# Layer norms whose variance is inverted before its root is taken, and a head norm that keeps its rows as four token quarters

## What is computed

```python
def layernorm(x, g, b):          # after the convolution, over 768 channels
    mu = jnp.mean(xf, axis=-1, keepdims=True)
    var = jnp.mean(jnp.square(xf - mu), axis=-1, keepdims=True)
    y = (xf - mu) * lax.rsqrt(var + LN_EPS)

def layer_norm(x, g, b):         # second block, over 1024 features
    ...
    return ((x32 - mu) * lax.rsqrt(var + LN_EPS) * g + b)

def rms_norm(x, g):              # over the 128 features of one head
    ms = jnp.mean(jnp.square(x32), axis=-1, keepdims=True)
    return (x32 * lax.rsqrt(ms + LN_EPS) * g)

def odd_mixer(...):
    o = diff_attention(q, k, v, lam)             # 8 heads of 128
    o = rms_norm(o, subln_g) * (1.0 - lambda_init)
    return o.reshape(b, s, DIFF_W) @ w_out

def second_block(...):
    for i in range(DEPTH):
        x = layer_norm(ALPHA * x + (1.0 + g_m) * y, ln_mix_g[i], ln_mix_b[i])
        h = x * (1.0 + sc_f) + sh_f
        y = swiglu(h, w_gate[i], w_up[i], w_down[i])
        x = layer_norm(ALPHA * x + (1.0 + g_f) * y, ln_ffn_g[i], ln_ffn_b[i])
```

## Time and profile before

| | |
|---|---|
| median of 3 runs | 2707.3 us (2707.06 to 2709.83) |
| the profiled execution's own time | 2703.21 us |
| its span in the trace | 2701.5 us |
| PE busy | 2552.7 us (94%), 12225 matmul records |
| DVE busy | 1549.3 us (57%), 2243 instructions |
| ACT busy | 1051.2 us (39%), 1596 instructions |
| granted clock of PE over the span | 0.97 of full |

### The profile page before, as it was taken

How to read it: one execution, slowest core, us unless ns; L and a number is a source line. 1 busy time by engine, 2 the same in 40 slices (tenths; PEclk the granted TensorE clock), 3 DMA queues, 4 the chain that set the end, 5 groups by cost and what they waited for, 6 DMA issues and landing times.

```text
span 2701.5 us, 30620 instructions
## 1 busy us (share of the span) xinstructions
PE 2552.7 (94%) x12225; PEld 1983.1 (73%) x12225; DVE 1549.3 (57%) x2243; ACT 1051.2 (39%) x1596; POOL 70.9 (3%) x145
## 2 busy tenths in 40 slices
PE   7798999999998999999999899999999989999998
PEld 5466777777865777777777567888878756788886
DVE  5876587777355467767657555333364765533335
ACT  5235332335445432323544535222244663522223
POOL 2000001010000000000000000000000000000000
PEclk9898999999999999999999999999999998999998
DMA  5121356563312235645231022333223111333321
GB/s 168 47 94 32 88 161 203 156 187 101 95 56 71 78 109 182 177 154 169 83 94 63 1 60 81 94 94 94 82 75 94 47 47 53 88 94 94 94 82 43
DMA packets 327836, 262.32 MB, mean 97 GB/s; under 512 B 13426, under 2 KB 312630, under 8 KB 327696
## 3 DMA queue, kind: packets, MB, share of 16 engines
q1 hardware_dynamic: 312000, 206.07, 25.8%
q0 software_dynamic: 15440, 54.25, 6.3%
q10 hardware_dynamic: 256, 0.07, 0.0%
HBM read 258.23 MB, written 2.12 MB: 96 GB/s over the span
## 4 chain that ended last, share of the span: by engine, by line
PE 71%; PEld 8%; DVE 8%; ACT 5%; issue 4%; DVEq 3%; DMA 1%; ACTq 0%; PEldq 0%
PE ps L396 43%; PEld ps L396 6%; PE ps L410 6%; PE ps L414 6%; PE ps L418 6%; PE ps L1308 2%; PE ps L1868 2%; DVE wL L362 2%; PE ps L1339 1%; PE ps L2348 1%; ACT tmpB L1384 1%; DVEq L896 1%; PE ps L1322 1%; DVE tmpA L905 1%; ACT tmpA L869 1%
## 5 line engine op out<-in xcount | busy, mean ns | idle before, releaser
L362 DVE TENSOR_TENSOR wL<-raw,wH 128x2048 fp32r<-128x2048 f32 (+1 forms) x185 | 415.3, 2245 | 120.0 <-ACT wH L348 113.9
L348 ACT ACTIVATE wH<-raw 128x2048 fp32r<-128x2048 f32 (+1 forms) x185 | 345.3, 1868 | 245.5 <-PE ps L396 106.2
L396 PE MATMUL ps<-hH,wH 128*128 128x512 f32 x1656 | 427.6, 400 | 5.0 <-issue 1.9
L396 PE MATMUL ps<-hL,wH 128*128 128x512 f32 x1656 | 427.6, 400 | 0.0
L396 PE MATMUL ps<-hH,wL 128*128 128x512 f32 x1656 | 424.6, 398 | 0.0
L396 PEld LDWEIGHTS ps<-hH,wH 128*128 128x128 f32 x1656 | 308.1, 188 | 87.1 <-issue 13.2
L396 PEld LDWEIGHTS ps<-hL,wH 128*128 128x128 f32 x1656 | 310.8, 189 | 79.5 <-issue 6.5
L396 PEld LDWEIGHTS ps<-hH,wL 128*128 128x128 f32 x1656 | 308.9, 188 | 77.2 <-issue 4.8
L869 ACT ACTIVATE tmpA<-ff_up,cols 128x512 f32<-128x512 f32 x88 | 67.0, 808 | 255.8 <-DVEq L896 255.8
L410 PE MATMUL ps<-gH,wH 128*128 128x512 f32 x480 | 153.3, 409 | 10.3 <-ACT wH L348 7.4
L931 DVE TENSOR_TENSOR tmpB<-ps,tmpB 128x512 f32<-128x512 f32 x44 | 30.4, 692 | 231.0 <-PE ps L396 231.0
(11 more groups left out here) (353 smaller groups left out, 3317.7 us busy)
## 6 DMA issues: line engine op xcount, KB each, us to landing
raw<-w_up SPq DMA_DIRECT2D x132, 512.0 KB, 5.2
mod_ring<-w_mod POOLq DMA_DIRECT2D x96, 512.0 KB, 4.5
raw<-w_down SPq DMA_DIRECT2D x32, 1024.0 KB, 5.3
raw<-w_gate SPq DMA_DIRECT2D x44, 512.0 KB, 4.0
raw<-w_down SPq DMA_DIRECT2D x16, 768.0 KB, 4.5
raw<-w_in_even SPq DMA_DIRECT2D x9, 1024.0 KB, 5.2
raw<-w_out SPq DMA_DIRECT2D x8, 1024.0 KB, 5.2
raw<-w_in_odd SPq DMA_DIRECT2D x16, 512.0 KB, 4.6
```

The costliest lines, as they stand in the source:

```text
L348: last = act.activation(wH[:, st.part, 0:st.size], raw[:, st.slot, 0:st.size], ACT.Copy)
L362: last = dve.tensor_tensor(wL[:, st.part, 0:st.size], raw[:, st.slot, 0:st.size], wH[:, st.part, 0:st.size].bitcast(F32), ALU.subtract)
L396: last = pe.matmul(dst, left, right, start=(t == 0 and k == 0), stop=(t == 2 and k == self.kt - 1))
```

## The change

In the five layer norms, epsilon is added to the variance by DVE's clipping instruction, which now does two operations; DVE inverts the variance right behind it; ACT then takes the root of the inverse, without a bias, and PE's second spread waits for ACT (`roots`) and no longer for DVE. The semaphore `centred` goes. The root mean square norm keeps its order.

The head norm uses the layer norms' layout: `sum_quarters` forms the means of a batch in four quarters of 32 rows and 128 columns, root and inversion work on 128 x 128 blocks, and `spread_quarters`, which has a new argument for the row, spreads head n from row n of each quarter. The tensor `pick` and the eight instructions that fill it (line 1575) go. The diff, cut to its core (`ConvNorm` has the same edits in its `tensor` and `scalar` methods as `NormParts`, and the reservations of `centred` are gone):

```diff
@@ -956,10 +955,11 @@
-        def spread_quarters(pe, bank, src):
+        def spread_quarters(pe, bank, src, row=0):
             for g in range(QT):
-                last = pe.matmul(ps[:, bank, g * P:g * P + P], ident[:, GROUP * g:GROUP * g + 1].broadcast_to([P, P]), src, start=True, stop=True)
+                r = GROUP * g + row
+                last = pe.matmul(ps[:, bank, g * P:g * P + P], ident[:, r:r + 1].broadcast_to([P, P]), src, start=True, stop=True)
             return last
...
@@ -1046,7 +1046,10 @@
                     spread_quarters(pe, 6, quarter_mean).then_inc(spread_out.sem, 1)
-                pe.wait_ge(inverted.sem, self.inverted0 + 1)
+                if self.bname:
+                    pe.wait_ge(roots.sem, self.root0 + 1)
+                else:
+                    pe.wait_ge(inverted.sem, self.inverted0 + 1)
                 spread_quarters(pe, 7, quarter_inv).then_inc(spread_out.sem, 1)
@@ -1054,8 +1057,8 @@
                     act.activation(quarter_square, ps[:, 6, 0:P], ACT.Square).then_inc(squares.sem, 1)
-                    act.wait_ge(centred.sem, self.centred0 + 1)
-                    act.activation(quarter_std, quarter_var, ACT.Sqrt, bias=eps_ln).then_inc(roots.sem, 1)
+                    act.wait_ge(inverted.sem, self.inverted0 + 1)
+                    act.activation(quarter_inv, quarter_std, ACT.Sqrt).then_inc(roots.sem, 1)
                 else:
@@ -1097,11 +1100,14 @@
                     dve.drain()
-                    dve.tensor_scalar(quarter_var, quarter_var, 0.0, None, ALU.max).then_inc(centred.sem, 1)
+                    dve.tensor_scalar(quarter_var, quarter_var, 0.0, LN_EPS, ALU.max, ALU.add)
+                    dve.drain()
+                    dve.reciprocal(quarter_std, quarter_var).then_inc(inverted.sem, 1)
                     dve.wait_ge(spread_out.sem, self.spread0 + 1)
                     self.centre(dve, 0)
-                dve.wait_ge(roots.sem, self.root0 + 1)
-                dve.reciprocal(quarter_inv, quarter_std).then_inc(inverted.sem, 1)
+                else:
+                    dve.wait_ge(roots.sem, self.root0 + 1)
+                    dve.reciprocal(quarter_inv, quarter_std).then_inc(inverted.sem, 1)
                 self.centre(dve, 1)
@@ -1494,6 +1500,9 @@
+            def quarters(self, batch):
+                return (acc, accq)[batch][:, 0:P]
+
             def mean(self, pe, batch):
@@ -1501,7 +1510,7 @@
                     pe.wait_ge(squares.sem, self.square0 + n + 1)
-                    last = pe.matmul(ps[0:32, (0, 6)[batch], :], pick_mean[:, n, :], difK[:, n, :], start=(n == heads[0]), stop=(n == heads[-1]))
+                    last = sum_quarters(pe, (0, 6)[batch], pick_mean[:, n, :], difK[:, n, :], n == heads[0], n == heads[-1])
                 last.then_inc(summed.sem, 1)
@@ -1509,7 +1518,7 @@
                     pe.wait_ge(normed.sem, self.normed0 + n - 1)
-                    pe.matmul(ps[:, self.bank(n), :], pick[0:8, n, :], (acc, accq)[batch][0:8, :], start=True, stop=True).then_inc(rows_in.sem, 1)
+                    spread_quarters(pe, self.bank(n), self.quarters(batch), n).then_inc(rows_in.sem, 1)
@@ -1528,7 +1537,7 @@
                 act.wait_ge(summed.sem, self.mean0 + batch + 1)
-                act.activation((acc, accq)[batch][0:32, :], ps[0:32, (0, 6)[batch], :], ACT.Sqrt, bias=eps_ln[0:32, :]).then_inc(roots.sem, 1)
+                act.activation(self.quarters(batch), ps[:, (0, 6)[batch], 0:P], ACT.Sqrt, bias=eps_ln).then_inc(roots.sem, 1)
@@ -1552,7 +1561,7 @@
                 dve.wait_ge(roots.sem, self.root0 + batch + 1)
-                dve.reciprocal((acc, accq)[batch][0:32, :], (acc, accq)[batch][0:32, :]).then_inc(inverted.sem, 1)
+                dve.reciprocal(self.quarters(batch), self.quarters(batch)).then_inc(inverted.sem, 1)
...
```

More of the change, by code:

```diff
@@ L188, in build @@
             difV = sb("difV", [P, QT, D], F32, main)
-            pick = sb("pick", [P, 8, P], F32, main)
             pick_mean = sb("pick_mean", [P, 8, 32], F32, main)
@@ L266, in build @@
         rotated, glu_done, ff_scaled = Signal("rotated", "dve"), Signal("glu_done", "dve"), Signal("ff_scaled", "dve")
-        parts, lows, centred = Signal("parts", "dve"), Signal("lows", "dve"), Signal("centred", "dve")
+        parts, lows = Signal("parts", "dve"), Signal("lows", "dve")
         ff_conv, ff_prod, ff_low = Signal("ff_conv", "dve"), Signal("ff_prod", "dve"), Signal("ff_low", "dve")
@@ L1023, in __init__ @@
                     self.mean0, self.square0 = means.reserve(1), squares.reserve(1)
-                    self.centred0, self.ready0 = centred.reserve(1), acc_ready.reserve(1)
+                    self.ready0 = acc_ready.reserve(1)
                 if self.modulated:
@@ L1574, in vector_slot @@
                     for n in range(8):
-                        dve.tensor_scalar(pick[:, n, :], ones[:, :], ident[:, n:n + 1], None, ALU.mult)
                         dve.memset(pick_mean[:, n, n:n + 1], 1.0 / P)
@@ L1908, in __init__ @@
                 self.sums0, self.square0, self.summed0 = sums_in.reserve(1), squares.reserve(NCONV + 1), summed.reserve(NCONV)
-                self.centred0, self.root0, self.part0 = centred.reserve(1), roots.reserve(1), parts.reserve(NCONV)
+                self.root0, self.part0 = roots.reserve(1), parts.reserve(NCONV)
                 self.mean0, self.spread0, self.inverted0 = means.reserve(1), spread_out.reserve(2), inverted.reserve(1)
```

## The result

The changed kernel took 2686.03 us (2683.41 to 2688.72, 4 runs), the kernel before beside it 2707.18 (2703.82 to 2709.83, 4 runs): a ratio of 0.9927 [0.9908, 0.9945], so it is faster. The forecast was 2695.8 with a range from 2690 to 2702. The direction was right, the gain larger than forecast: 21.2 us between the medians, 19.8 by the ratio (14.9 to 24.9), against 11.5. The two profiled executions are 14.5 us apart: 2688.72 us with a span of 2687.0, against 2703.21 with 2701.5.

The account below looks back on a forecast made before the run. PE with its weight loads was taken to bound the kernel, 79% of the chain ending last. Terms 2.6 + 3.8 + 0.3 + 2.4 - 0.2 + 1.35 + 1.3 = 11.5 us, off the 2707.3 median: 2695.8 us, range 2690 to 2702.

Parts of the forecast that it names:

- Layer norms (-2.6): Five layer norms: the second spread starts 0.52 us sooner after the subtraction in each, 2.6 us less.
- Rival 4: The layer norms give nothing, because something other than the spread sets when first matmuls begin: 2699.7 us, chance 0.08.
- Mean of batch 0 (-3.8): Odd attention tail: quarter matmuls cut PE's mean from 5.92 to 2.15 us, 3.8 us less, bounds 3.0 and 4.4.
- Rival 3: Quarter matmuls don't overlap in the head norm, so both means keep their times: 2702.2 us, chance 0.04.
- Root and inversion of batch 0 (-0.3, -2.4): Head norm: root from 0.68 to 0.40 us, inversion from 3.33 to 0.94, PE's idle 2.57 shrinking to about 0.2.
- Spreads (+0.2): Head norm: three pairs of spreads on the path cost 0 to 0.8 us more, taken as 0.2.
- mean of batch 1 (-1.35): Inside the output product, PE's mean goes from 1.84 to 0.5 us; its root and inversion stay hidden.
- The clock (-1.3): Odd attention tail: less idle time and fuller matmuls raise PE's clock, 1.3 us less, within -3.3 to +5.3.
- the second stretch: 2240.73 to 2246.50 us, PE busy at 1.2 GHz after 8-row spreads; running at 2.4 GHz it would give 2.65 us.
- rival 1: The clock stays up through the whole odd attention tail: 13.5 us less, 2693.8 us, chance 0.12.
- Rival 2: The clock is lost in slots 28 to 30, as 5.9 us of dense work go: 5.3 us lost, 2702.4 us, chance 0.12.
- Rival 5: Slower: the clock, once down, isn't given back in the output product: 2716.6 us, chance 0.04.

Follow-up runs that it names:

- e5_gap: The changed kernel with one more DVE inversion, of 128 x 384, ahead of batch 0's inversion: 2688.58 us, ratio 0.9927 to the kernel before.
- e3_rows128: The kernel before, with only its head-norm spreads reading all 128 rows, the added selector rows being zero: 2697.41 us, ratio 0.9968.
- e0_again: The changed kernel unaltered, measured once more beside the kernel before: 2689.64 us, ratio 0.994.
- e7_early: The changed kernel with ACT's high and DVE's low parts of the heads a slot later, DVE's head products ahead of its maxima: 2687.3 us, ratio 0.9925.
- e9_nobias: The kernel before in its old order, with epsilon added by DVE's clip in layer norms and ACT's root without bias: 2709.68 us, measured once.
- e2_heads: The kernel before with the quarter layout in the head norm alone, layer norms as before: 2691.69 us, ratio 0.9953.
- e1_norms: The kernel before with the new order in the five layer norms alone, head norm as before: 2700.01 us, ratio 0.9981.

## Why the prediction was right, and where it fell short

- **Layer norms (-2.6): right, 2.8.** The path, its order and the hand-over were as worked out; the root was 0.09 us shorter. The table load of the convolution's norm had the 0.7 us of cover that was forecast: ACT idles 0.73 us behind it (236.89). Rival 4, no gain from the norms, is out: line 1115 moved with the spread.
- **Mean of batch 0 (-3.8): right.** Logits of unit 28 start 3.7 us earlier. Rival 3, quarter matmuls without overlap, is out. By the Trainium skill, "TensorE: Matmul & The Clock Gate", section on the back-to-back issue gap, with its 62 ns for each matmul where hardware decoding is off, the estimate for the 48 records is 3.0 us. They took 2.27, part of it at 1.2 GHz (mean clock 0.64). The measurement does not bear that case out here; whether decoding was off, no run shows.
- **Root and inversion of batch 0 (-0.3, -2.4): right** where they stand: 4.0 us in all at unit 30's logits, 2.4 more at the first spread. What the prediction did not have is the wait that PE runs into next, 3.50 us for the scaling of unit 31: it let the scaling come earlier "by the same time". By e5_gap, 2.55 us more of inversion cost 0.4 at the end of the tail, so the 2.4 us count there for little as long as PE waits for that scaling anyway.
- **Spreads (+0.2) and mean of batch 1 (-1.35): near.** At the full clock a pair takes 1.95 to 2.05 us, so the spreads cost nothing; between the mean of batch 1 and head 6's product 1.3 us more were gained.
- **The clock (-1.3): the step that failed.** "I take half of the second stretch" was mis-sized. The tail lost 11.56 us, the terms without the clock sum to 7.85 (3.8 + 0.3 + 2.4 - 0.2 + 1.35 = 7.65, and 0.2 that the spreads did not cost), which leaves 3.7 for the clock. That is a remainder and not a measurement: where the inversion's 2.4 us are lost again in the new wait, the clock's part is larger. It comes out as rival 1, "the clock stays up through the whole tail", with its 3.3 us, though I gave it 0.12. The second failure in the term is its ceiling: the prediction let the clock give back 3.3 us at most, read from the one profile of before, while widening the rows alone gave 8.7 us (5.7 to 11.6) in e3_rows128, of which its profile shows 3.5 in the tail. So of the two reasons that the prediction named, the 128 rows are shown to matter by themselves; for less idle time nothing is shown, since in e5_gap the clock was down before the gap came. Against rival 1 stood the gap in which ACT loads tables. It is still there, 2.08 us, and in this execution the clock stood through it; in e0_again, e5_gap and e7_early the logits behind it took 1.65 us at the low clock. With that and its third pair at 1.2 GHz, e0_again's tail was 2.7 us longer, so that of the 3.7 us 1.0 is left. Rival 2, the clock lost in slots 28 to 30, came in part in e0_again: slot 30 alone, from its logits to the first spread 2.93 us for the 1.95 of the other execution, 1.0 us for the 5.3 that I gave it. Rival 5 is out: the output product from the mean of batch 1 to the spread of head 6 took 14.8 us in both (2237.96 to 2252.74, 2239.19 to 2253.97).
- **The starting point: the larger part of the miss.** The forecast lies 9.8 us above the measured median. The profiled pair accounts for 3.0 of them (14.5 us gained for 11.5); the other 6.7 lie between the pair's 14.5 and the medians' 21.2. The step is "on that median the forecast is 2707.3 - 11.5": it went from one execution, 4.1 us below the median, and took its difference over. The 16 and the 9 runs of before spread over 10.7 and 5.9 us, and e9_nobias' tail of 61.34 us shows that an execution can have less of the high clock than the profiled one. The mean granted clocks say so too: 0.975 over the 4 runs of the changed kernel, 0.969 over the 16 runs of before, 0.9736 over the 5 of e0_again, 0.973 over the 6 of e3_rows128, while the profiled pair has 0.970 and 0.973. So in the median the clock differs more than in the profiled pair, and the gain is larger: 19.8 us by the first comparison, 16.2 by the repeat, against 14.5. Where in the program the other executions gained it, no profile shows.

By these numbers the kernel's gain is 16 to 20 us: about 3 from the norms, up to 7.9 from shorter work and waits on PE's path, and the rest from the clock. The rest is had by subtraction. It fits the 8.7 us of e3_rows128 in size, but the parts don't simply add: 7.65 and 8.7 would be 16.3 for the head norm, and e2_heads measured 12.7 (9.5 to 16.2). How the clock's part divides between 8-row matmuls and idle time in the new form stays open. What decides in one execution whether the clock falls in ACT's gap was not found. A spread from 32 rows at a time in the new form, which would have tested the rows there, wasn't tried.

The sign that the prediction gave for its tail, 8 to 9 us shorter, was passed with 11.56. Its sign of being wrong, a window at 0.50 that stood at 1.00, did not occur in the changed kernel's profile and did in e0_again's, at the logits of unit 30.

## What to carry to other kernels

Keep per-token statistics of a layout on the partitions as four quarters: both DVE's inversion and ACT's root are paid by the column (inversion 0.94 us for 128 columns on 128 partitions, 3.33 for 512 on 32; root 0.37 and 0.68), and at the full clock the shorter matmuls of the spreads cost no more for it (1.95 us a pair for 2.06). When an edit touches what PE does around idle time, count the stretches at 1.2 GHz near it as a term of their own, whose size changes from run to run, and give it its full range rather than half; and carry a difference of two profiled executions over to a median only with the spread of the runs beside it. Widening selector matmuls of 8 rows with zeros is worth a try: here it gave 8.7 us. When a stall goes, look for the chain that PE will then catch up with: here 2.38 idle us went, and two slots later 3.50 stood where 0.20 had been.

## What the runs showed of the hardware that was not expected

- Behind spreads that read 8 rows the clock stayed low although PE was busy: in the earlier trace rows 3.71 us of them were followed by another 4.14 busy us at 0.50, and a second pair at full clock by a fall. The same instructions over 128 rows took the same 3.78 us at the low clock, but the clock rose within the next 1.6 us and stayed up to the end of the tail, and the whole kernel took 0.9968 of its time. By the clock records of the ten traces the clock came back 8.0, 8.2 and 21.9 us after the start of the first pair where it had 8 rows (before, e1_norms, e9_nobias), and 3.5 to 5.5 us after it in the five profiles with 128 rows whose first pair ran low.
- ACT's root of 128 x 128 from SBUF takes 0.40 us with a bias of one value for each partition and 0.31 without (e9_nobias). With the bias and its input in PSUM, in the changed head norm, it took 0.37.
- The clock stood at 1.00 through 3.50 us in which PE did nothing (2228.37 to 2231.87), and in e0_again, the same code, it fell within an idle time of 2.09 us (logits of unit 30). In these traces the length of an idle time of two or three us alone does not say whether the clock falls.
